# Four chunks of the next expert's weights in a second place, moved by VectorE, in a mixture-of-experts loop

## The reference, cut to what matters

```python
logits = xt @ p['w_router'] + p['b_router']
top_val, top_idx = lax.top_k(logits, TOP_K)            # TOP_K = 4, N_EXPERTS = 32
gates = jax.nn.softmax(top_val, axis=-1)
...
def expert_block(args):
    e, x_b = args
    gu = x_b @ w_gu[e] + b_gu[e]                       # (tokens, 1024) @ (1024, 2048)
    gate = jnp.minimum(gu[..., ::2], SWIGLU_LIMIT)
    up = jnp.clip(gu[..., 1::2], -SWIGLU_LIMIT, SWIGLU_LIMIT)
    return ((up + 1.0) * (gate * jax.nn.sigmoid(SWIGLU_ALPHA * gate))) @ w_dn[e] + b_dn[e]
...
x = x + mx[5] * rms_norm(moe_ffn(hf, p), g_post_ffn[l])
```

## Time and profile before

| | us |
|---|---|
| median of 3 runs | 3154.93 (3154.46 to 3165.39) |
| the profiled execution's own time | 3159.1 |
| its span, first to last instruction | 3157.3 |
| TensorE matmul busy | 2608.4 (83%) |
| VectorE busy | 1028.8 (33%) |
| ScalarE busy | 759.4 (24%) |
| GpSimd busy | 366.5 (12%) |
| the loop's matmuls at L1353, 3008 of them | 668.1 |
| the loop's matmuls at L1379, 1504 of them | 344.9 |

### The profile page before, as it was taken

One profiled execution on the slowest core, in us unless ns is written; L12 is line 12 of the kernel. 1 busy time (PEld: TensorE's weight loads), 2 busy tenths in 40 slices (PEclk: granted clock), 3 DMA queues, 4 the chain that ended last, 5 costly groups with the idle time before them and its releaser, 6 DMA issues. The chain is left out here.

```text
span 3157.3 us, 51833 instructions
## 1 busy us (share of the span) xinstructions
PE 2608.4 (83%) x19262; PEld 1298.6 (41%) x19262; DVE 1028.8 (33%) x2288; ACT 759.4 (24%) x1718; POOL 366.5 (12%) x339
## 2 busy tenths in 40 slices
PE   6778585847679995598988989998999499779998
PEld 2446363636454442333333333333333144356444
DVE  1263636373165523322222222222222512443012
ACT  2123333333051002122222222222222201354000
POOL 0031212212051000000000000000000200244000
PEclk8888797978889998799999999999999699887999
DMA  5100000000216423589999999399969421001112
GB/s 201 55 25 23 6 23 6 11 14 4 81 54 242 171 80 134 222 343 388 387 391 389 389 421 391 152 387 425 387 268 377 147 89 63 19 2 54 53 54 79
DMA packets 114086, 553.29 MB, mean 175 GB/s; under 512 B 12912, under 2 KB 16496, under 8 KB 62352
## 3 DMA queue, kind: packets, MB, share of 16 engines
q1 hardware_dynamic: 97184, 510.21, 40.1%
q10 hardware_dynamic: 10608, 19.91, 1.9%
q0 software_dynamic: 6144, 20.98, 1.8%
HBM read 736.12 MB, written 16.52 MB: 238 GB/s over the span
## 5 line engine op out<-in xcount | busy, mean ns | idle before, releaser
L1353 PE MATMUL moe_gu_ps<-expert_w,xgT 128*64 128x512 f32 x3008 | 668.1, 595 | 40.7 <-PEq L1318 40.6
L1353 PEld LDWEIGHTS moe_gu_ps<-expert_w,xgT 128*64 128x64 f32 x3008 | 252.4, 137 | 448.0 <-issue 448.0
L1379 PE MATMUL moe_down_ps<-expert_w,actT 128*64 128x512 f32 x1504 | 344.9, 597 | 54.4 <-PEq L1318 54.0
L1439 DVE TENSOR_TENSOR biased<-moe_gu_ps,b_gu 128x512 f32<-128x512 f32 x94 | 65.0, 692 | 618.5 <-DVEq L1318 618.5
L1379 PEld LDWEIGHTS moe_down_ps<-expert_w,actT 128*64 128x64 f32 x1504 | 116.5, 136 | 222.2 <-issue 222.2
L1400 ACT ACT_TABLE_LOAD x47 | 60.3, 1283 | 385.5 <-ACTq L1318 385.5
L1858 PE MATMUL ahead_ps<-hT,x 128*128 128x256 f32 (+1 forms) x288 | 127.1, 538 | 23.6 <-PEq L57 23.6
L1333 POOL COPY tokens<-token_of 128x1 uint32 x47 | 8.6, 183 | 1042.6 <-POOLq L1318 1042.6
L1280 ACT ACTIVATE xgT<-moe_xg_ps,ffn_shift,ffn_gain 128x64 f32<-128x64 f32 x384 | 119.2, 424 | 41.0 <-PE moe_xg_ps L1274 41.0
L1404 ACT COPY actT<-moe_act_ps 128x256 f32<-128x256 f32 x94 | 35.0, 372 | 376.0 <-ACTq L1318 376.0
L386 PE MATMUL b2p_ps<-b_w,b_hT 128*128 128x512 f32 (+1 forms) x320 | 121.1, 541 | 2.0 <-PEq L57 2.0
(11 more groups left out here) (687 smaller groups left out, 3734.1 us busy)
## 6 DMA issues: line engine op xcount, KB each, us to landing
expert_w<-in_w_experts SPq DMA_DIRECT2D x576, 1024.0 KB
late_w<-in_w_late SPq DMA_DIRECT2D x12, 2048.0 KB, 8.5
b_w<-in_w_in SPq DMA_DIRECT2D x10, 2048.0 KB, 7.6
ada_w<-in_w_ada SPq DMA_DIRECT2D x6, 2048.0 KB, 12.8
slot_rows<-yb ACTq DMA_DIRECT2D x94, 128.0 KB, 6.3
mix_w<-in_w_in_tok SPq DMA_DIRECT2D x5, 2048.0 KB, 10.4
x<-in_w_rkv SPq DMA_DIRECT2D x5, 1536.0 KB, 7.3
mix_w<-in_w_out SPq DMA_DIRECT2D x2, 2048.0 KB, 8.5
```

Source lines behind the costliest of these rows:

```text
L1353: last = nc.tensor.matmul(ps_gu[SLOTS * j:SLOTS * j + SLOTS, half, :], xgT[:, k, :], w[:, i, at:at + 512], start=(k == 0), stop=(k == KD - 1),
L1379: last = nc.tensor.matmul(ps_dn[SLOTS * j:SLOTS * j + SLOTS, :], actT[:, half, q, SLOTS * a:SLOTS * a + SLOTS], w[:, i, at:at + 512], star ...
L1439: step(nc.vector.tensor_tensor(biased[:, :], ps_gu[:, half, :], b_gu[:, half, :], ALU.add))
```

## The change

Four more places of 1 MB are added behind the 12 (`STAGED = 4`). They hold chunks 0 to 3 of the expert after the one at work. In each turn, after its last product, VectorE waits for each of the four and copies it into place 0 to 3 (`to` is 0 in the last turn of an expert); in a turn that is not an expert's last, `to` is 12 and the copy goes onto its own place, so that the semaphores stay in step. TensorE waits for chunks 0 to 3 on the copies (`moved`) and for the others on their arrival, as before. SP no longer calls chunks 0 to 3 into their places: in an expert's last turn it calls chunks 4 to 11 of the next expert, and between them chunks 0 to 3 of the one after that into the second place, in the order 4, 5, 6, 7, 8, s0, 9, s1, 10, s2, 11, s3 (s for the second place). The table gets two more rows for it, and `route_stage` 11 more operations on VectorE's chain and two more small DMAs. To make room, the normalized tokens get a tile of their own that is freed before the loop (`ffn_xn`), `ffn_y` and the weight ring are allocated after the loop, and `of_expert` shares the space of the late modulation's columns.

```diff
@@ ffn_block
-        y = sb("ffn_y", [P, NT_X, D])
-        moving = ffn.enter_context(ExitStack())
+        xn = routing.enter_context(nc.sbuf_tensor("ffn_xn", [P, NT_X, D], F32))
...
         moving.close()
+        ring = WeightRing(nc, "b2_w", whole)
+        y = ffn.enter_context(nc.sbuf_tensor("ffn_y", [P, NT_X, D], F32))
@@ route_stage, SP
-                sp.dma_start(table[0:1, :], experti[:, 0:1]).then_inc(s["table"], 16)
-                sp.wait_ge(s["table"], 16)
+                for j in range(3):
+                    sp.dma_start(table[0:1, j, :], experti[:, j:j + 1]).then_inc(s["table"], 16)
+                sp.wait_ge(s["table"], 48)
@@ route_stage, VectorE (the one step at L1158 becomes two, and ten are new)
+                step(nc.vector.scalar_tensor_tensor(tmp[:, :], starts[:, :], part[:, 0:1], ends[:, :], ALU.is_equal, ALU.mult))
+                step(nc.vector.tensor_reduce(many[:, 0:1], tmp[:, :], AX.X, ALU.max))
...
@@ ExpertWeights
-        self.w = held.enter_context(nc.sbuf_tensor("expert_w", [P, CHUNKS, 2 * D], F32))
+        self.w = held.enter_context(nc.sbuf_tensor("expert_w", [P, CHUNKS + STAGED, 2 * D], F32))
@@ experts, SP
+                first = sp.value_load(table[0:1, 0, 0:1], min_val=0, max_val=N_EXP - 1)
+                second = sp.value_load(table[0:1, 1, 0:1], min_val=0, max_val=N_EXP - 1)
+                for i in range(STAGED):
+                    sp.dma_start(w[:, CHUNKS + i], weights.source[second, i], cond=(second != first)) \
+                        .then_inc(arrived[i], 16)
                 with sp.Fori(0, turns) as v:
...
-                    for i in range(CHUNKS):
+                    def load_rest(i):
                         takes(sp, s["last_used"] if i == CHUNKS - 1 else s["used"])
                         sp.dma_start(w[:, i], weights.source[after, i], cond=(after != here)).then_inc(arrived[i], 16)
+                    for i in range(STAGED, 2 * STAGED):
+                        load_rest(i)
+                    for i in range(STAGED):
+                        load_rest(2 * STAGED + i)
+                        takes(sp, stage_free)
+                        sp.dma_start(w[:, CHUNKS + i], weights.source[following, i],
+                                     cond=(following != after)).then_inc(arrived[i], 16)
@@ experts, TensorE
-                        if k % 2 == 0:
+                        if k % 2 == 0 and i < STAGED:
+                            takes(pe, moved)
+                        elif k % 2 == 0:
                             takes(pe, arrived[i], 16)
@@ experts, VectorE
-                with dve.Fori(0, turns):
+                with dve.Fori(0, turns) as v:
+                    to = dve.value_load(table[0:1, 2, bass.ds(v, 1)], min_val=0, max_val=CHUNKS)
...
+                    for i in range(STAGED):
+                        takes(dve, arrived[i], 16)
+                        step(nc.vector.tensor_copy(w[:, bass.ds(to + i, 1), :], w[:, CHUNKS + i:CHUNKS + i + 1, :]))
+                        nc.vector.sem_inc(moved, 1)
+                        nc.vector.sem_inc(stage_free, 1)
```

More of the change, by code:

```diff
@@ L661, in _ @@
                 nc.vector.tensor_copy(shift[:, :], g.ada[:, 24:32, 0]).then_inc(s["done"], 1)
-        norm_turn_stage(nc, "ffn", tiles, None, [y[:, m] for m in range(NT_X)], hT,
+        norm_turn_stage(nc, "ffn", tiles, None, [xn[:, m] for m in range(NT_X)], hT,
                         lambda m, k: (gain[:, k:k + 1], shift[:, k:k + 1]), g.eps_col[:, 0:1], g.ident[:, :],
                         early=weights.load_first)
-        route_stage(nc, tables, g, hT, ones, y, rows, weight, slot_of, of_expert, token_of, table, n_blocks)
+        route_stage(nc, tables, g, hT, ones, xn, rows, weight, slot_of, of_expert, token_of, table, n_blocks)
         routing.close()
@@ L1156, in _ @@
                 step(nc.vector.tensor_tensor(starts[:, :], ends[:, :], blocks[:, :], ALU.subtract))
-                step(nc.vector.tensor_scalar(many[:, 2:3], many[:, 2:3], -1.0, part[:, 0:1], ALU.add, ALU.min))
+                last_block = many[:, 3:4]
+                step(nc.vector.tensor_scalar(last_block, many[:, 2:3], -1.0, None, ALU.add))
+                step(nc.vector.tensor_scalar(many[:, 2:3], last_block, part[:, 0:1], None, ALU.min))
                 step(nc.vector.tensor_scalar(tmp[:, :], starts[:, :], many[:, 2:3], None, ALU.is_le))
@@ L1163, in _ @@
                 step(nc.vector.tensor_reduce(expert[:, 0:1], tmp[:, :], AX.X, ALU.add))
-                nc.vector.tensor_copy(experti[:, :], expert[:, 0:1]).then_inc(s["expert"], 1)
+                step(nc.vector.scalar_tensor_tensor(tmp[:, :], starts[:, :], part[:, 0:1], ends[:, :], ALU.is_equal, ALU.mult))
+                step(nc.vector.tensor_reduce(many[:, 0:1], tmp[:, :], AX.X, ALU.max))
+                step(nc.vector.tensor_tensor(many[:, 0:1], many[:, 0:1], part[:, 0:1], ALU.max))
+                step(nc.vector.tensor_scalar(many[:, 0:1], many[:, 0:1], last_block, None, ALU.min))
+                step(nc.vector.scalar_tensor_tensor(tmp[:, :], starts[:, :], many[:, 0:1], iota[:, 0:N_EXP],
+                                                    ALU.is_le, ALU.mult))
+                step(nc.vector.scalar_tensor_tensor(tmp[:, :], ends[:, :], many[:, 0:1], tmp[:, :], ALU.is_gt, ALU.mult))
+                step(nc.vector.tensor_reduce(expert[:, 1:2], tmp[:, :], AX.X, ALU.add))
+                step(nc.vector.tensor_scalar(tmp[:, :], ends[:, :], -1.0, part[:, 0:1], ALU.add, ALU.is_equal))
+                step(nc.vector.tensor_reduce(many[:, 1:2], tmp[:, :], AX.X, ALU.max))
+                step(nc.vector.tensor_scalar(expert[:, 2:3], many[:, 1:2], -float(CHUNKS), float(CHUNKS), ALU.mult, ALU.add))
+                nc.vector.tensor_copy(experti[:, :], expert[:, 0:3]).then_inc(s["expert"], 1)
                 step(nc.vector.tensor_scalar(starts[:, :], starts[:, :], float(SLOTS), None, ALU.mult))
@@ L1284, in modulate, with takes, _ @@
             last.then_inc(xgT_made, 1)
+        def takes(engine, signal, n=1):
+            engine.wait_ge(signal, n).then_inc(signal, -n)
         with stage(nc, "moe_start", "tokens", "xg_turned", "set", "rows_set", pool_dma=(gathered,)) as (s, block):
+            @block.sync
+            def _(sp):
+                for i in range(STAGED):
+                    takes(sp, arrived[i], 16)
+                    sp.sem_inc(moved, 1)
             @block.vector
@@ L1355, in gate_up @@
                                                     skip_group_check=True)
-                            if half == 1 and k == 0 and j == 0:
-                                last.then_inc(s["used"], 1)
-                        if k % 2 and k < KD - 1:
+                        if k % 2 and k < KD - 1 and i >= STAGED:
                             last.then_inc(s["used"], 1)
@@ L1407, in _ @@
                 with act.Fori(0, turns) as v:
-                    here = act.value_load(table[0:1, bass.ds(v, 1)], min_val=0, max_val=N_EXP - 1)
-                    after = act.value_load(table[0:1, bass.ds(v + 1, 1)], min_val=0, max_val=N_EXP - 1)
+                    here = act.value_load(table[0:1, 0, bass.ds(v, 1)], min_val=0, max_val=N_EXP - 1)
+                    after = act.value_load(table[0:1, 0, bass.ds(v + 1, 1)], min_val=0, max_val=N_EXP - 1)
                     sigmoid()
```

38 lines of the change are left out of this document (22 added, 16 removed).

## The result

| | before | after |
|---|---|---|
| median, us | 3159.76 (3154.46 to 3165.39) | 3232.59 (3223.84 to 3236.82) |
| ratio | | 1.0227, interval 1.0207 to 1.0247 |
| profiled execution's own time, us | 3159.1 | 3223.8 |
| span of it, us | 3157.3 | 3222.0 |

A forecast was written before the change was run, and what follows sets the result against it. The prediction took TensorE's matmuls to set the pace, with late turns waiting for the weight queue. Landings 38.6, clock 21.8 and routing 2.7 summed to +63.1 us: 3222 us for the profiled execution, 3218 for the median, range 3170 to 3250.

The forecast's parts named there:

- The late start: In the loop, SyncE's first call of a row comes at 9.11 us instead of 2.83, so every row starts 6.28 us later.
- The landing term: In the loop, each chunk 11 lands 3.7 us later; over seven rows of three and four of two, +38.6 us.
- Moved allocations: 0: Across the kernel, moving the buffers' allocations was priced at 0 us.
- the chunk saved: In a row, 35 chunks carried up to the last expert's chunk 11 instead of 36: -2.6 us.
- The clock term: At 11 row ends, TensorE falls to half clock after long waits, 1.98 us each: +21.8 us, bounds 0 and 44.
- The copies: VectorE's four copies per turn, 1.75 us each with the wait behind, stay hidden: 0, bounds 0 and 47 x 1.0 us.
- Routing: Ahead of the loop, 11 more steps at 0.245 us on the chain TensorE waits for: +2.7 us, bounds 2 and 5.
- SyncE: In its loop turn, twelve calls as before and one table read more, while it waits for place 4 anyway: 0.
- Rival B: In the loop, s0 to s2 don't delay chunk 11: 3129 us, or 3143 with seven clock falls; chance 0.10.
- Rival A: At row ends, the waits leave TensorE's clock at 2.4 GHz: 3196 us; chance 0.17.
- D: In the loop, a start less late than 6.28 us or one staged chunk behind 11, no falls: 3175 us; chance 0.08.
- C: In the loop, the clock stays low twice as long, or copies end 1 us late in some turns: 3240 us up; chance 0.10.

The follow-up runs named there:

- e3: The kernel before, with only the start moved: SyncE calls chunks 0 to 3 only when place 4 is free; 3229.14 us, ratio 1.0219.
- after_again: The changed kernel run once more, unaltered, for a second trace of the clock; 3235.99 us, ratio 1.0239.
- e4: The changed kernel with VectorE's copies cut to 64 of 2048 columns, calls and waits the same; 3230.41 us, ratio 1.0229.
- e1: The changed kernel with chunks 8 to 11 called ahead of s0 to s3; 3200.13 us, ratio 1.0140.
- e2: The changed kernel with calls ordered 8, s0, 9, 10, 11, s1, s2, s3, so one staged chunk ahead of chunk 11; 3199.67 us, ratio 1.0138.

## Why the prediction was right, point by point

**The late start** was right, and is the cause: SyncE's first call at T + 9.20 for the 9.11 forecast, and e3 shows that this alone, with neither a second place nor a copy, makes a loss of the same size.

**The landing term was too small.** Forecast was +3.7 us for each chunk 11. The first's is +4.1, the second's +5.0, the third's +5.5. In the rows of three where the fall of the clock meets only chunk 10 and so costs nothing, the loss is 12.6 us (106.0 us long), in two of the three such rows of two some 4.6, and the term is 7 x (12.6 - 7.3) + 4 x 4.6 = 55.5 us, not 38.6. The records show where most of this comes from, and the forecast had put it at nothing ("Moved allocations: 0"). Two chunks with no other traffic between them land 2.45 us apart in the kernel before and in e3, and 2.49 in every kernel with sixteen places, also with short copies (medians of over 180 pairs in each trace). Over 35 chunks that is 1.2 us. Whether the greater tile or the moved allocations bring it, no run separates. e3 gives a cross-check: with 36 chunks the third landing is 104.6 there, with 35 of them 104.2 here. So the chunk saved, priced at 2.6, shows as 0.4 against e3: the slower chunks take 1.2 of it, and 0.5 is that e3 calls its first four at once and has the second land 2.5 us behind the first instead of 2.9. The rest, some 0.4 us, is open.

**The clock term was too large.** Falls at the row ends were forecast, and they come: half clock follows waits of 2 us and more, though not each of them (2.21 us ahead of chunk 9 leave it at full). The section "HAM oscillation — how this bites in real kernels" of the Trainium skill's page "TensorE: Matmul & The Clock Gate" has short bursts of matmuls with waits for DMA between them fall back to half clock, and this trace agrees (0.58 over the stretch shown), while e3 with its short waits holds 1.00. But 1.98 us for each of 11 ends, 21.8 in all, had the fall paid at the start of the next turn. In the trace it comes within the late turn: in 8 of 11 row ends chunk 10 alone is hit, and a wait for chunk 11 follows that takes it in. The clock costs 61.1 - 55.5 = some 6 us in this execution; in after_again the rows lose 3.5 us more.

So the sum, 60.4 for 61.1 us, is right by **two errors that cancel**: 17 us too little on the landings, 16 too much on the clock. The mechanisms, a late start and a falling clock, were right; that the number is so near is luck.

**The copies** came out as priced, again by two errors that cancel: 1.24 us for a copy, under the lower bound of 1.5, and 0.55 for the wait behind it where 0.25 was taken, together 1.77 us from one to the next for 1.75. They are hidden, as forecast (e4). **Routing**: +2.6 for +2.7. **SyncE**: 0, as forecast. By the medians the change costs 73 us for the 63 forecast; after_again, 6.5 us longer than the first trace, has 3.5 of them in the loop and 3.3 behind it, where nothing was changed.

**Rival B** (s0 to s2 don't delay chunk 11) fails by the rows of two, 74.7 us and not 70.1, and by e1, where calling them later moves the first row's third landing from 104.1 to 96.3: 2.6 us for each of three chunks. **Rival A** (the clock stands) fails by the 0.58 of the stretch shown, though its price for the landings was as mis-sized as the forecast's. **D** (a start less late, or a staged chunk that slips behind 11) isn't there, with the start at 9.20; its 3175 leaves out the routing's 2.7. **C** had it that the copies bind: they don't here, but in e1 and e2 they do, by a wait that the prediction didn't see. It asked only when the copies end, and not what they wait for in a turn that needs none.

## What to carry to other kernels

More room for a prefetch is worth what it does to two times: when the queue's first call can be made, and how many transfers stand ahead of the last one that is wanted; the changed kernel, with four extra places and a start 6.3 us later, lost 2.3%, and the ring of sixteen places, with the early start kept, won 0.8%. Where a copy or a semaphore is kept "in step" in turns that don't need it, ask what it waits for there. Price a clock fall only where no wait stands behind it.

## What the runs showed of the hardware that was not expected

- A VectorE copy of 128x2048 float32 within on-chip memory, to a place given by a register, takes 1.24 us, less than twice the 753 ns of an operation with one tile input on 1024 columns.
- A like lateness costs clock or not by how it is spread: eight waits of 0.4 to 1.3 us in a turn hold 1.00 (e3), a single one of 2.00 us ahead of chunk 10 is followed by half clock (3.39 us for its matmuls). Length alone doesn't decide it: in e1_eleven_first 2.17 us ahead of chunk 0 leave it at full (1.94 us).
- With sixteen places for the weights instead of twelve a chunk of 1 MB takes the queue 2.49 us instead of 2.45, in all ten traces of such kernels and whatever the length of VectorE's copies.
- A transfer can be held up by one of its sixteen parts: in the ring's row from 1607.09 fifteen parts of the third expert's chunk 11 land within 2.4 us, and the last one lands 6.8 us behind the first.
- Four copies of TensorE's turn, 31 jumps between them, show no cost (70.08 us for a row of two for 70.09 before).
